# First block's scan: product steps of the second half mixer in pairs, at every second level of scores

## The reference, cut to what matters

```python
proj = xn @ w_in + b_in
o_h = (hgrn2_scan(q_h, k_fwd, v_h, lf_fwd)
       + flip_seq(hgrn2_scan(flip_seq(q_h), flip_seq(k_bwd), flip_seq(v_h), flip_seq(lf_bwd))))
# in one chunk of the scan:
diff = cum[:, :, :, None, :] - cum[:, :, None, :, :]
decay = jnp.exp(jnp.where(tril[:, :, None], diff, -jnp.inf))
scores = jnp.einsum('bhtd,bhsd,bhtsd->bhts', qc, kc, decay)
state = jnp.exp(cum_last)[..., None] * state + jnp.einsum('bhsd,bhse->bhde', k_dec, vc)
```

## Time and profile before

| | us |
|---|---|
| median of 3 runs | 1923.15 |
| lowest and highest | 1923.02, 1923.83 |
| span of the profiled execution | 1921.1 |
| total time of the profiled execution | not listed apart; by the median some 2.05 above the span |

### The profile page before, as it was taken

How to read it: one execution, slowest core, us unless ns; L and a number is a source line. 1 busy time by engine, 2 the same in 40 slices (tenths; PEclk the granted TensorE clock), 3 DMA queues, 4 the chain that set the end, 5 groups by cost and what they waited for, 6 DMA issues and landing times.

```text
span 1921.1 us, 23196 instructions
## 1 busy us (share of the span) xinstructions
PE 1865.3 (97%) x9394; PEld 1385.0 (72%) x9394; DVE 794.1 (41%) x1193; ACT 555.0 (29%) x1124; POOL 991.9 (52%) x566
## 2 busy tenths in 40 slices
PE   7999998999999999999999999999999999999988
PEld 6888887778788888888777888888854444434446
DVE  4466668651414401422566485635241222211234
ACT  5535548342412200211223453332231000000025
POOL 6597866757377877887575796437600000000021
PEclk9999999999999999999999999999999999999999
DMA  6221122323123223322332233102889999999991
GB/s 210 79 77 44 45 66 99 132 68 108 45 77 97 93 96 99 99 99 95 105 88 77 79 88 97 56 33 88 344 362 426 429 426 428 427 427 428 422 371 62
DMA packets 82777, 335.87 MB, mean 175 GB/s; under 512 B 6512, under 2 KB 8304, under 8 KB 67568
## 3 DMA queue, kind: packets, MB, share of 16 engines
q1 hardware_dynamic: 79296, 322.47, 44.7%
q10 hardware_dynamic: 3376, 11.93, 1.7%
HBM read 328.08 MB, written 6.29 MB: 174 GB/s over the span
## 4 chain that ended last, share of the span: by engine, by line
PE 85%; DMA 7%; DVE 4%; ACT 2%; POOL 1%; issue 1%; SPq 0%; DVEq 0%; ACTq 0%; POOLq 0%
PE bank L638 54%; PE bank L1972 11%; DMA shared<-in_w_exp_up 3%; PE bank L2009 3%; PE bank L815 2%; DMA rows<-in_w_exp_up 2%; PE bank L1991 2%; DMA arena<-in_w_exp_up 1%; PE bank L659 1%; PE bank L1100 1%; PE bank L2126 1%; PE bank L1490 1%; PE bank L1697 1%; PE bank L2249 1%; PE bank L1086 1%
## 5 line engine op out<-in xcount | busy, mean ns | idle before, releaser
L638 PE MATMUL bank<-shared_r 128*128 128x512 f32 (+2 forms) x3312 | 759.7, 386 | 13.3 <-POOL shared_r L696 4.9
L638 PEld LDWEIGHTS bank<-shared_r 128*128 128x128 f32 x3312 | 598.0, 189 | 136.8 <-POOL shared_r L678 8.8
L677 POOL TENSOR_TENSOR shared_r<-shared,small 128x1024 fp32r<-128x1024 f32 (+1 forms) x154 | 300.5, 1951 | 296.8 <-PE bank L638 288.0
L678 POOL TENSOR_TENSOR shared_r<-shared,shared_r 128x1024 fp32r<-128x1024 f32 (+1 forms) x154 | 374.3, 2430 | 12.1
L677 POOL TENSOR_TENSOR spare_r<-arena,small 128x1024 fp32r<-128x1024 f32 x2 | 3.8, 1898 | 474.8 <-DMA arena<-in_w_ple_gate 474.8
L1972 PE MATMUL bank<-arena 128*64 128x512 f32 x624 | 185.0, 593 | 4.9 <-DMA rows<-in_w_exp_up 2.7
L638 PE MATMUL bank<-shared_r,arena_r 128*128 128x512 f32 x768 | 174.4, 389 | 0.0
L638 PEld LDWEIGHTS bank<-shared_r,arena_r 128*128 128x128 f32 x768 | 144.1, 188 | 29.9
L1972 PE MATMUL bank<-shared,arena 128*64 128x512 f32 x608 | 133.1, 593 | 8.4 <-DMA shared<-in_w_exp_up 8.0
L1972 PEld LDWEIGHTS bank<-arena 128*64 128x64 f32 x624 | 59.4, 137 | 92.0 <-issue 89.8
L1972 PEld LDWEIGHTS bank<-shared,arena 128*64 128x64 f32 x608 | 45.3, 137 | 93.1 <-issue 92.5
(11 more groups left out here) (457 smaller groups left out, 2581.5 us busy)
## 6 DMA issues: line engine op xcount, KB each, us to landing
shared<-in_w_in SPq DMA_DIRECT2D x80, 512.0 KB, 3.5
arena<-in_w_exp_down SPq DMA_DIRECT2D x11, 2048.0 KB, 29.7
arena<-in_w_exp_gate SPq DMA_DIRECT2D x10, 2048.0 KB, 35.2
shared<-in_w_exp_gate SPq DMA_DIRECT2D x10, 2048.0 KB, 20.7
shared<-in_w_exp_up SPq DMA_DIRECT2D x10, 2048.0 KB, 29.8
arena<-in_w_exp_up SPq DMA_DIRECT2D x9, 2048.0 KB, 21.8
shared<-in_w_up SPq DMA_DIRECT2D x32, 512.0 KB, 3.6
shared<-in_w_down SPq DMA_DIRECT2D x32, 512.0 KB, 3.5
```

What stands on the lines that cost most here:

```text
L638: ins = pe.matmul(dst, W_, x_, start=first, stop=final)
L677: link(pool.tensor_tensor(hi, raw(p), small[:, 18:19].to_broadcast([P, hi.shape[1]]), ALU.add))
L678: pool.tensor_tensor(lo, raw(p), hi.bitcast(F32), ALU.subtract).then_inc(S_("w_split"), 1)
```

## The change

One condition in `hg_pe`. Before, one step of `proj_m` runs behind every level but L1. After, two steps run behind L2, L4 and L6, and none behind the others. The number of steps in a chunk stays six.

```diff
             bank_ready(ins, n)
-            if what == "level" and x not in (1,):
-                run_steps(steps, 1)
+            if what == "level" and x in (2, 4, 6):
+                run_steps(steps, 2)
 
     def hg_steps(m, l):
```

## The result

The change makes the kernel slower: 1930.28 us (median of 5 runs, 1928.93 to 1931.26) against 1923.02 us (5 runs). The ratio is 1.0036, 95% interval 1.0025 to 1.0046. In microseconds that is 7.3 where 4.6 was forecast; the range given (1922.6 to 1931.0) held it.

The account below looks back on a forecast made before the run. TensorE was taken to bound the first block's scan; waits of 3.3, 1.3 and 0.8 us less 0.8 us gave 4.6 us on 1923.15, so 1927.8 us, range 1922.6 to 1931.0.

Parts of the forecast that it names:

- The scan bounds, and its end goes into the total: First block's scan: TensorE busy 145.46 of 147.53 us; any shift of the scan's end enters the total one to one.
- No gain or loss of the pairs themselves: Steps run in pairs on TensorE: between 0 and 2.4 us of gain, taken as 0.2 us.
- L2 of the odd chunks: Chunks 1, 3, 5, 7: level L2 waits uncovered for its operand behind GpSimd's split; 3.3 us, with 0.1 for L1.
- the rule that stood beside the prediction's sum: VectorE and GpSimd block each other: L0's product in chunks 1, 5, 7 ends with the split; sum 5.5 us.
- L2 of the even chunks: Chunks 2, 4, 6: level L2, tied to GpSimd's split, waits 0.6, 0.4 and 0.3 us for chunks 2, 6, 4; 1.3 us.
- L4: Level L4, with no step ahead, waits for VectorE's product behind the copy of out: 0.6 us in chunk 4, 0.8 in all.
- The end: Chunk 7: the last but one step's wait for VectorE's evacuation is covered once it comes behind L6; -0.6 us.
- That the pairs gain 2.4 us: Rival in the scan: pairs give their full gain and old waits go; not slower, likelier -2 us, 1921.2 us; chance 0.09.
- A pile-up of the splits: Rival at chunks 2, 4, 6: splits fall behind their steps; about +8.8 us, 1932 us; chance 0.05.
- the chain did not give way: Rival denied here: VectorE and GpSimd get earlier turns, only waits of chunks 3 and 5 stay; 0 to +2.4 us; chance 0.14.

Follow-up runs that it names:

- run 3: Kernel before with only the step behind L0 moved behind L2, so one pair per chunk: 1937.38 us, ratio 1.0075.
- run 11: Kernel before with only L5's step moved behind L6, so one pair per chunk: 1922.07 us, ratio 0.9993.
- run 9: Changed kernel with GpSimd's split behind L2's subtractions in odd chunks and VectorE's mask copy of L2 ahead of out: 1926.93 us, ratio 1.0021.
- run 6: Changed kernel with GpSimd making the split's low part behind L2's subtractions in the odd chunks: 1926.85 us, ratio 1.0023.
- run 8: Changed kernel with VectorE's mask copy of L2 made ahead of out instead of behind L4's product: 1930.30 us, ratio 1.0038.
- run 5: Changed kernel with dummy matmuls on TensorE ahead of the waits of L1 and L2 in chunks 1, 2, 3, 4, 5 and 7: 1929.07 us, ratio 1.0030.
- run 4: The kernel of run 3 with two dummy matmuls ahead of the waits of L1 and L2 in chunks 1 to 7: 1931.25 us, ratio 1.0045.

## Why the prediction was right or wrong

Right in direction, mechanism and place; too small in size, 4.6 us against 7.3. The range held the result, though L4's bank and the clock, which filled it up, were not what it was made for.

- **The scan bounds, and its end goes into the total.** Right: +7.6 us at the load of `mem`, +7.0 us in the span.
- **No gain or loss of the pairs themselves.** Right, taken at 0.2 us. A pair takes 2.83 to 2.85 us against 2 x 1.46; own and state, which now follow a level, take 0.94 us where it was 0.89. Run 3 (few pairs, most loss) and run 11 (pairs, no loss) show it from both sides, and run 9's sum leaves 0.2 us.
- **L2 of the odd chunks.** Right: K to L2 forecast at 8.3, 9.45, 8.85 and 8.3 us, measured 8.45, 9.49, 8.97 and 8.53, and all odd chunks together 3.5 us net where 3.3 was forecast. The mechanism needs a correction. The chain through GpSimd's queue was taken as the only one, and L2's product was to start some 0.2 us earlier after K, once the mask copy of L6 was out of its way. In chunks 1 and 7 VectorE's own row of products and copies is as long (run 6), and it did not move. It hangs on L0's product, which ends with the split. VectorE in the kernel before, then VectorE and GpSimd in the changed kernel, chunk 1:

```profile
149.29 0.88 DVE L952 TENSOR_TENSOR arena<-arena 128x256 f32<-128x256 f32 x1
...
148.01 2.26 DVE L952 TENSOR_TENSOR arena<-arena 128x256 f32<-128x256 f32 x1
...
147.60 2.39 POOL L696 TENSOR_TENSOR shared_r<-shared,shared_r 128x1024 fp32r<-128x1024 f32 x1 [3.67 <-ACT shared_r L687]
```

  The product ends at 150.27, 0.28 us after the split (149.99), and L1 is 0.34 us late. Before, it began later and was shorter, and ended at 150.17, 0.28 us after its split (149.89) as well: 5.5 us behind K both times. That own came earlier won nothing. This is the rule that stood beside the prediction's sum, from the Trainium skill, SBUF — State Buffer, Who interferes with whom: a VectorE instruction with two SBUF inputs is blocked while GpSimd reads. The trace agrees in all of chunks 1, 3, 5 and 7; in chunks 3 and 5 it is L1's product that is held.
- **L2 of the even chunks.** Right: in chunk 2 L2 was tied to the split and starts at 171.42 us, as it did before, though TensorE was there sooner. In size too high: L1 and L2 of chunks 2, 4 and 6 are 1.5 us late, but 0.8 us of delay at L0 to L2 of these chunks in the kernel before is gone, so 0.7 net where 1.3 was forecast.
- **L4.** The term that was mis-sized most: 0.8 us forecast, 2.5 measured. Chunk 4 was hit (0.6). For the others the prediction looked only at the product, and not at the bank that L4 claims, which VectorE frees behind that product; run 8 removed the waits on L961 by moving the mask copy. 1.0 us of it, in chunk 5, goes with the fall of the clock: L4's product came late and was held by a split (1.55 us long, from 237.82), which it escapes in run 5.
- **The clock.** Missing from the sum: 1.5 us in the profiled execution, some 2 with what it brings about at L4 and takes back in chunk 6 (run 5). The granted clock of 1.00 in the earlier trace rows was read as a constant, while the change was about to lengthen the idle time. How much of it is in the medians is open: the changed kernel's five executions have mean clocks of 0.995 to 0.997, and those of the kernel before beside the experiments 0.994 to 0.998, with 0.996 in the middle of both, and 0.001 of the span is already 2 us.
- **The end.** Right: both evacuation waits are gone, 1.2 and 0.8 us from start to start where 1.03 and 0.6 were taken.
- **The rivals.** That the pairs gain 2.4 us found no support (runs 3 and 9), and the rule of the Trainium skill, Perfetto Trace Analysis, Matmul Optimizations, that matmuls should go back to back in batches, bought nothing here: the trace has less than 0.1 us for a pair, and while the batches grew, TensorE's idle time grew too, from 2.07 to 6.28 us. A pile-up of the splits was not seen, and the chain did not give way.

The sum by measured terms: L1 and L2 4.2 us net (4.6 forecast), L4 2.5 (0.8), the clock 1.5 (none), the evacuation of chunk 7 -0.8 (-0.6), the pairs about 0 (-0.2). That makes 7.4 of the 7.5 us of the scan. How many such stretches at the lower clock the other four executions had inside the scan is open.

## What to carry to other kernels

Independent work between dependent steps of an in-order engine is cover for the operand that comes next; moving it costs just where the next operand is ready last. List for each consumer when its operand is ready against when the engine would get there, and also who frees its PSUM bank. If such a move leaves the bound engine waiting more often, count the clock too: here it made some 6 of the 13 us that the scan lost in the worst case.

## What the runs showed of the hardware

- The granted clock of TensorE fell inside the scan behind waits that are short in themselves: after 1.2 us of wait in chunk 5 of the changed kernel, after 0.73 and 0.31 us in chunk 2 of run 3. The stretches lasted 3.4 or 6.8 us at half the clock. With dummy matmuls of some 0.25 us each in place of the idle time it stayed up (run 4; in run 5 for the one profiled execution). Not every wait brings a fall: in chunk 3 of the changed kernel L2 was 1.8 us late, and the clock stayed; in run 8 it fell after the same wait in the same chunk, and stayed in chunk 5.
- Moving one step of a chunk's six (run 3) cost more, 14.6 us, than moving three (the change), 7.3 us. The waits of the levels were about as long in sum (8.9 and 9.2 us). Of the 5.7 us between the ends of the two scans the clock makes 4.5 (6.0 against 1.5), and 2.0 are the two evacuation waits, which stay in run 3; some 0.8 go the other way. Why the clock fell for longer there is open; in run 3 L1 and L2 waited in each of the chunks 1 to 7, and it fell in the two chunks in which L0 had waited 0.9 and 1.0 us before them.
- A VectorE product that meets a GpSimd split ended 0.28 us after the split in each case looked at (1.84, 2.26, 2.04 and 1.97 us long, against 0.71 alone), however much of the split was left when it began: one that began 0.6 us before the split's end was 0.88 us long.
